# Delta rule by 64x64 tiles: the transpose of X comes from VectorE's block transpositions instead of products

## The reference, cut to what matters

```python
gcum = jnp.cumsum(g, axis=-1)
decay = jnp.exp(jnp.where(incl, gcum[..., :, None] - gcum[..., None, :], -jnp.inf))
kb = k * beta[..., None]
lower = jnp.where(strict, jnp.einsum('bhncd,bhnsd->bhncs', kb, k) * decay, 0.0)
tmat = lax.linalg.triangular_solve(eye + lower, eye, left_side=True, lower=True, unit_diagonal=True)
u = tmat @ (v * beta[..., None])
w = tmat @ (kb * jnp.exp(gcum)[..., None])
...
v_new = u_c - w_c @ s
o = qd_c @ s + a_c @ v_new
s * jnp.exp(gl_c)[..., None, None] + jnp.swapaxes(kd_c, -1, -2) @ v_new, o
```

## Time and profile before

| | us |
|---|---|
| median of 3 runs | 3926.3 |
| the runs | 3925.33 to 3931.67 |
| the profiled execution, its own time | 3924.58 |
| its span, first to last instruction | 3922.4 |
| the delta rule's chunks in it | 1394.3 to 1630, and a tail until 1640 |

### The profile page before, as it was taken

One profiled execution on the slowest core, in us unless ns is written; L12 is line 12 of the kernel. 1 busy time (PEld: TensorE's weight loads), 2 busy tenths in 40 slices (PEclk: granted clock), 3 DMA queues, 4 the chain that ended last, 5 costly groups with the idle time before them and its releaser, 6 DMA issues. The chain is left out here.

```text
span 3922.4 us, 55157 instructions
## 1 busy us (share of the span) xinstructions
PE 3588.2 (91%) x23086; PEld 2879.1 (73%) x23086; DVE 1959.0 (50%) x3107; ACT 844.8 (22%) x1650; POOL 1440.3 (37%) x701
## 2 busy tenths in 40 slices
PE   6897988999989978878999899899999899899998
PEld 3684567888877867757888576788888576788887
DVE  5797653223446444474233367863243377853342
ACT  3213512110011233201100344422000344421001
POOL 2331043226554223115455222235455222245454
PEclk9898999999999977889999899999999899999999
DMA  5443312212113100112332231123332322223322
GB/s 172 150 151 135 129 43 76 65 59 62 63 49 91 41 3 4 67 42 72 97 97 81 67 80 49 49 72 95 96 97 75 84 60 53 55 76 97 97 92 81
DMA packets 399811, 306.40 MB, mean 78 GB/s; under 512 B 11292, under 2 KB 367462, under 8 KB 398983
## 3 DMA queue, kind: packets, MB, share of 16 engines
q1 hardware_dynamic: 397464, 302.37, 25.6%
q10 hardware_dynamic: 2095, 0.44, 0.1%
HBM read 296.48 MB, written 6.29 MB: 77 GB/s over the span
## 5 line engine op out<-in xcount | busy, mean ns | idle before, releaser
L450 POOL TENSOR_TENSOR low<-raw,high 128x1024 fp32r<-128x1024 f32 (+1 forms) x437 | 1049.7, 2403 | 1828.6 <-DVE high L356 1828.6
L519 PE MATMUL scores<-high 128*128 128x512 f32 (+1 forms) x1944 | 743.1, 382 | 72.2 <-DVE low L704 31.8
L519 PE MATMUL scores<-low,high 128*128 128x512 f32 (+1 forms) x1944 | 729.4, 375 | 0.0
L519 PE MATMUL scores<-high,low 128*128 128x512 f32 (+1 forms) x1944 | 727.7, 374 | 0.0
L356 DVE CAST high<-raw 128x1024 fp32r<-128x1024 f32 (+1 forms) x437 | 394.4, 903 | 504.1 <-PE scores L519 261.1
L519 PE MATMUL bank<-high 128*128 128x512 f32 (+1 forms) x1480 | 541.6, 366 | 0.2
L519 PE MATMUL bank<-low,high 128*128 128x512 f32 (+1 forms) x1480 | 538.8, 364 | 0.0
L519 PE MATMUL bank<-high,low 128*128 128x512 f32 (+1 forms) x1480 | 538.1, 364 | 0.0
L519 PEld LDWEIGHTS scores<-high 128*128 128x128 f32 x1944 | 376.7, 194 | 154.7 <-POOL low L450 54.2
L519 PEld LDWEIGHTS scores<-high,low 128*128 128x128 f32 x1944 | 375.6, 193 | 65.9
L519 PEld LDWEIGHTS scores<-low,high 128*128 128x128 f32 x1944 | 377.2, 194 | 62.0 <-issue 1.0
(11 more groups left out here) (663 smaller groups left out, 5143.3 us busy)
## 6 DMA issues: line engine op xcount, KB each, us to landing
raw<-in_mlp_w SPq DMA_DIRECT2D x128, 512.0 KB, 3.9
raw<-in_w_in SPq DMA_DIRECT2D x76, 512.0 KB, 3.9
ring<-in_ada_w SPq DMA_DIRECT2D x32, 1024.0 KB, 7.5
raw<-in_w_gate SPq DMA_DIRECT2D x44, 512.0 KB, 3.8
raw<-in_w_up SPq DMA_DIRECT2D x44, 512.0 KB, 3.9
raw<-in_w_down SPq DMA_DIRECT2D x40, 512.0 KB, 3.5
mix<-in_ada_w SPq DMA_DIRECT2D x16, 1024.0 KB, 6.5
raw<-in_od_w_in SPq DMA_DIRECT2D x29, 512.0 KB, 3.9
```

The source lines that it names most:

```text
L450: pool.tensor_tensor(tile(low, u), tile(raw, u), tile(high, u).bitcast(F32), ALU.subtract)\
L519: mm = pe.matmul(out(p), stationary, moving, start=(k0 + k == 0 and i == 0), stop=(k0 + k == job.kc - 1 and i == len(pairs) - 1))
```

## The change

- Tiles of levels 0 to 4 are the two 64x64 blocks of the diagonal for each head in place of four of 32x32: 8 matmuls for a product. X, XT and `part` are 128x256 instead of 128x128, and so are the operations of VectorE that write all of them; the updates that `subtract` reads are 128x128 instead of 128x64. The masks and the identity become 64 wide (384 KB and 32 KB instead of 160 and 16).
- `second_turned` is gone at levels 1 to 4, and `subtract_turned` with it. In its place VectorE transposes X into XT by 32x32 blocks (`turn`) after each subtraction; until level 4 X has nothing outside the 32x32 blocks of the diagonal. X itself begins as VectorE's transposition of XT, so `second` at level 0 is gone.
- Level 5 is a level like the others, but keeps both updates: `part` on VectorE masks it, `second_turned` and `second` follow, and `subtract_turned` and `subtract` on VectorE.
- `square`, `wide`, `copy_part`, `copy_wide_part`, `place_square`, `place_corners` and `last_corner` are gone. ScalarE copies the two 64x64 blocks of each head into `inverse`, the part of level 6 and its corner.
- GpSimd's `place_blocks` is gone, and with it its waits for XT; three of GpSimd's waits for its own operations are gone, and `exponents` waits for an earlier `mask_decays`.
- VectorE's `advance` of both streams moves from behind `attention` to between the parts and the subtractions of level 5; `subtract_both` takes one stream after the other.

```diff
             def first(s, k, lv):
+                pe.wait_ge(s.xt_ready, 6 * k + lv)
+                for h in range(HEADS):
+                    for to, of in zip(halves, halves) if lv < 6 else ((s.earlier, s.later),):
+                        mm = pe.matmul(s.level[to, h, :], by_head(s.low)[of, h, to], s.XT[of, S(h)], start=True, stop=True)
+                mm.then_inc(s.firsts, 1)
...
             def second(s, k, lv):
-                if lv == 0:
-                    pe.wait_ge(s.part_ready, 5 * k + 1)
+                pe.wait_ge(s.part_ready, 6 * k + lv + 1)
+                pe.wait_ge(s.x_ready, 6 * k + lv)
                 for h in range(HEADS):
-                    for e, l in s.steps[0:1] if lv == 5 else ((b, b) for b in range(4)):
-                        mm = pe.matmul(s.level_x[R(l), h, :], s.part[R(e), B(h)], ident32[R(e), :] if lv == 0 else s.X[R(e), B(h)],
-                                       start=True, stop=True)
+                    for r in halves if lv < 5 else (s.earlier,):
+                        mm = pe.matmul(s.level_x[r, h, :], s.part[r, S(h)], s.X[r, S(h)], start=True, stop=True)
                 mm.then_inc(s.seconds, 1)
...
             def level(k, lv):
                 for s in both:
-                    second_turned(s, k, lv)
+                    if lv >= 5:
+                        second_turned(s, k, lv)
                     if lv < 6:
                         second(s, k, lv)
...
+            def copy_last_part(s, k):
                 act.wait_ge(s.firsts, 6 * k + 6)
+                act.activation(by_block(s.part)[s.earlier, :, :], s.level[s.earlier, :, :], ACT.Copy).then_inc(s.last_part, 1)
+
+            def place_blocks(s, k):
+                if k == 0:
+                    act.wait_ge(s.cleared, 2)
+                act.wait_ge(s.xt_ready, 6 * k + 6)
+                for r in halves:
+                    act.activation(by_head(s.inverse)[r, :, r], by_block(s.XT)[r, :, :], ACT.Copy).then_inc(s.diagonal, 1)
+
+            def place_corner(s, k):
+                act.wait_ge(s.seconds_turned, 2 * k + 2)
+                act.activation(by_head(s.inverse)[s.earlier, :, s.later], s.level_turned[s.earlier, :, :], ACT.Copy, scale=-1.0)\
+                    .then_inc(s.corner_ready, 1)
...
             def begin(s, k):
-                dve.wait_ge(s.seconds, 6 * k + 1)
-                if k:
-                    dve.wait_ge(s.square_ready, k)
-                dve.tensor_tensor(by_block(s.X), eye, s.level_x, ALU.subtract).then_inc(s.x_ready, 1)
+                dve.wait_ge(s.xt_ready, 6 * k + 1)
+                dve.transpose(s.X[:, :], s.XT[:, :]).then_inc(s.x_ready, 1)
+
+            def turn(s, k, lv):
+                dve.wait_ge(s.x_ready, 6 * k + lv + 1)
+                dve.transpose(s.XT[:, :], s.X[:, :]).then_inc(s.xt_ready, 1)
...
             def subtract_both(k, lv):
                 for s in both:
-                    subtract_turned(s, k, lv)
-                for s in both:
+                    if lv == 5:
+                        subtract_turned(s, k, lv)
                     subtract(s, k, lv)
+                    if lv < 5:
+                        turn(s, k, lv)
...
                     subtract_both(k, 4)
+                    for s in both:
+                        part(s, k, 5)
+                if has:
+                    for s in both:
+                        advance(s, j)
+                if more:
+                    subtract_both(k, 5)
                 if has:
                     for s in both:
                         attention(s, j)
-                        advance(s, j)
```

More of the change, by code:

```diff
@@ L2342 @@
         "query_raised": "ScalarE: of the queries (latent)", "keys_decayed": "ScalarE: keys decayed to the chunk's end",
-        "new_copied": "ScalarE: the new values", "square_ready": "ScalarE: X's blocks in the earlier 64 rows",
-        "wide_part": "ScalarE: the parts of levels 5 and 6 (2)", "corners": "ScalarE: corners of level 5 (3)",
+        "new_copied": "ScalarE: the new values", "last_part": "ScalarE: the part of level 6",
+        "corner_ready": "ScalarE: the corner of the inverse's last level", "diagonal": "ScalarE: blocks of the inverse (2)",
         "ends_ready": "VectorE: exponents", "low_ready": "VectorE: low",
-        "part_ready": "VectorE: the level's part of (X low) transposed (5: levels 0 to 4)",
-        "x_ready": "VectorE: X (5)", "xt_ready": "VectorE: X transposed (5)",
-        "xt_final": "VectorE: the corner of the inverse's last level", "attn_ready": "VectorE: attention (latent)",
+        "part_ready": "VectorE: the level's part of (X low) transposed (6: levels 0 to 5)",
+        "x_ready": "VectorE: X (6)", "xt_ready": "VectorE: X transposed (6)",
+        "attn_ready": "VectorE: attention (latent)",
         "rhs_ready": "VectorE: right-hand side", "state_ready": "VectorE: the state", "out_stored": "VectorE: the output (latent)",
@@ L2351 @@
         "values_scaled": "GpSimd: beta v", "decays_masked": "GpSimd: decays of the attention (latent)",
-        "query_ready": "GpSimd: decayed queries (latent)", "diagonal": "GpSimd: blocks of the inverse (4: later rows, earlier rows)",
-        "cleared": "GpSimd: the tiles that begin with zeros (3)"}
+        "query_ready": "GpSimd: decayed queries (latent)", "cleared": "GpSimd: the tiles that begin with zeros (2)"}
     def __init__(self, direction, banks, tiles, sems):
@@ L2369, in __init__ @@
         self.heads = slice(direction * HEADS, (direction + 1) * HEADS)
-        self.steps = [(0, 1), (2, 3)] if direction == 0 else [(3, 2), (1, 0)]
         self.earlier, self.later = (slice(0, 64), slice(64, P))[::1 if direction == 0 else -1]
         by_block = lambda t: t.rearrange("p (h n) -> p h n", h=HEADS)
-        self.level, self.level_turned = (by_block(self.level_bank[:, 128 * i:128 * i + 128]) for i in range(2))
-        self.level_x = by_block(self.gram_bank[:, 0:128])
-        self.corner = by_block(self.level_bank[:, 128:384])
+        self.level, self.level_turned = (by_block(self.level_bank[:, 256 * i:256 * i + 256]) for i in range(2))
+        self.level_x = by_block(self.gram_bank[:, 0:256])
     def sums_of(self, k):
@@ L2890, in last_corner @@
-            def last_corner(s, k):
-                dve.wait_ge(s.seconds_turned, 6 * k + 6)
-                dve.tensor_scalar(by_head(s.inverse)[s.earlier, :, s.later], s.corner[s.earlier, :, :], -1.0, None, ALU.mult)\
-                    .then_inc(s.xt_final, 1)
+                dve.wait_ge(s.seconds, 5 * k + lv)
+                dve.wait_ge(s.x_ready, 6 * k + lv)
+                rows = slice(0, P) if lv < 5 else s.earlier
+                own = s.half(s.X, lv, 0)[rows, :, :]
+                dve.tensor_tensor(own, own, s.half(s.gram_bank[:, 0:256], lv, 0)[rows, :, :], ALU.subtract).then_inc(s.x_ready, 1)
@@ L2986, in _ @@
                         lower(s, k + 1)
-                if more:
-                    for s in both:
-                        last_corner(s, k)
             for s in both:
```

171 lines of the change are left out of this document (43 added, 128 removed).

## The result

The kernel after takes 3878.76 us (median of 4 runs, 3873.06 to 3880.86), the kernel before 3928.99 beside it (3925.33 to 3932.06): ratio 0.987, 95% interval 0.9853 to 0.9887. A second comparison gave 0.9874, 0.9852 to 0.9897. It is 50 us faster; the forecast was 3901, 25 us faster.

The account below looks back on a forecast made before the run. TensorE was taken as bound by its work plus idle time from instruction supply and a lowered clock. Gaps -38, path +28 and clock -15 gave -25 us, so 3901 us, with a range of 3870 to 3930.

Parts of the forecast that it names:

- the band of 3886 to 3917: Whole kernel time in the main forecast outcome, given a chance of 0.62.
- The gaps: TensorE's "issue" idle time at 32x32 products, read as instruction supply: 38 of 39.1 us would go.
- the path: Time added in the delta rule by larger VectorE operations, transpositions and longer TensorE steps: 28 us.
- the clock's term: TensorE's half-level time, 2(1-share) times chunk length, 110 us in all, would fall by 45 us: -15 us.
- my price of 0.34: Chunk time per microsecond at half clock level, from comparing chunks 3 and 4 with the same work: 0.34 us.
- the clock goes to full nearly everywhere: Rival: TensorE's clock is full nearly throughout the chunks, clock term -37, kernel time 3879 us; chance 0.13.
- the level: One level with two 128x128 products between its halves: from 3.86 to 4.52 us, 0.66 more.
- The transposition itself: VectorE's transposition of 128x256 fp32 after each subtraction: taken as 0.42 us.
- The corner: ScalarE's corner copy at level 6, in three chunks without outputs: may come 0.5 us late, inside the 28.
- The advance of the state: VectorE's update between level 5's parts and subtraction: at most 1.7 us, hidden under TensorE's work.
- The signs named beforehand: Stage signs: "issue" under 5 us, 28 fewer transfers, chunks 34 to 36 us, share above 0.82, VectorE up a third.
- The signs of being wrong: Transposition waits over 1 us a level, clock share under 0.72, or 64x64 steps of 0.9 us.

Follow-up runs that it names:

- run 3: Kernel after plus 19 one-column matmuls before each `first` of levels 2 to 5 and `second` of levels 1 to 4, restoring the earlier record count: 3954.08 us.
- run 5: Kernel after with padding of 6 matmuls of 64 columns at each place where another version had 19 of one column: 3899.17 us.
- run 2: Kernel before, keeping 32x32 tiles, with VectorE's transpositions of X at levels 0 to 4 in place of products: 3866.89 us.
- run 4: Kernel after with every transposition of X into XT at levels 1 to 4 done twice, one after the other: 3901.29 us.
- run 6: Kernel after with ScalarE copying the inverse's blocks before the last level's part instead of after it: 3869.99 us.
- run 1: Kernel after's 64x64 tiles alone, with X's transpose still updated by products as in the kernel before: 3884.4 us.

## Why the prediction was right, and where its sizes were off

The measured time lies in the stated range of 3870 to 3930, but not in the band of 3886 to 3917 that had 0.62: the gain was twice the forecast one. The gaps and the path came out as summed; the clock's term was too small.

**The gaps (forecast -38).** Right. They are gone: 39.1 us on the lines of the earlier trace rows, 43.7 with the other tile products. That they are the supply of instructions I had read from counts; the traces now show it in time. The four gaps of TensorE in 17 us of the kernel before, and the DMA activity in slices of 0.425 us over the same 17 us:

```profile
1404.47 0.39 PE L2489 MATMUL bank<-XT,low 32*32 32x32 f32 x23 [1.83 <-issue]
...
1408.12 0.49 PE L2521 MATMUL bank<-X,part 32*32 32x32 f32 x21 [2.25 <-issue]
...
1412.01 0.54 PE L2521 MATMUL scores<-X,part 32*32 32x32 f32 x24 [1.76 <-issue]
...
1415.84 0.55 PE L2489 MATMUL bank<-XT,low 32*32 32x32 f32 x25 [1.91 <-issue]
```
```profile
DMA  1000000010000000020000000010000000010000
GB/s 39 0 0 0 0 0 0 0 39 0 0 0 0 0 0 0 0 39 0 0 0 0 0 0 0 0 39 0 0 0 0 0 0 0 0 39 0 0 0 0
...
q8 instruction: 5, 0.08, 2.1%
```

The transfers start at about 1402.0, 1405.4, 1409.2, 1413.1 and 1416.9 us, 3.4 to 3.9 us apart, and each gap ends 2.5 to 2.8 us after one starts. Runs 3 and 5 then show that the gaps come with the number of instructions, and run 3 that the rate counts and not the sum: with the records and transfers of before, in a stage 32 us longer, it has 10.3 us of gaps. A transfer brings about 128 matmul records (6,672 / 52), each with its weight load, so one in 3.6 us is 36 of them a microsecond. A level with two 128x128 products asks for 208 in 3.86 us before (54 a microsecond) and has the most gaps; 224 in 5.57 in run 3, with one product (40); 144 in 3.97 in run 2 (36), with few; and 80 in 4.79 after (17), with none. A short burst above the rate passes without a gap: 143 records in the 3 us of the first stretch shown in run 3 (48). The Trainium skill, "Runtime: NRT & Kernel Launch", instruction fetch mechanics, holds the fetch to be hidden; that is so for the kernel after and not for the 32x32 levels of before.

**The clock (forecast -15).** This is the mis-sized term. I took 45 us off the half-level time, on the ground that each level keeps 0.7 us of idle time. 89 went (110 to 21), at my price of 0.34 a gain of 30 us, and 40 us at 0.45, which is run 3's 39 / 86 if all that is left over there is clock. The rival "the clock goes to full nearly everywhere" had 3879, which is the time measured; the outcome is nearer to that rival than to the forecast. The step that failed is the one from idle time to clock. What I could not know, run 4 shows: waits of 0.45 to 0.9 us between bursts leave the clock at 1.00, while the waits of 1.6 us that run 6 takes away, the gaps of 2 us before and some gaps of 1 us (run 3) have a half-level stretch of several microseconds behind them. The Trainium skill, "TensorE: Matmul & The Clock Gate", section on oscillation, has the array throttled by waits between bursts: the longer waits here bear that out, the short ones do not. What separates a wait of 0.9 us in run 4 from the gap of 1.0 in run 3, and the one wait of 1.57 us in run 1 from its two others, stays open; so does why the gap of 1.61 us of the kernel before that ends at 1607.00 us has no such stretch behind it.

**The path (forecast +28).** -46.9 is -43.7 of gaps, -30 of clock and so +27 of path; with the clock at 0.45 it would be +37. The split between the two is no sharper than that. Its largest part is the level, 0.93 us longer, forecast 0.66 (4.79 for 4.52): the two `first` products took 1.27 us (1541.61 to 1542.88) where I had 0.92, since a 64x64 step is 0.51 us and not 0.46, and the second direction's starts 0.66 us after the first's, when its own transposition is done. That is 18.6 us in 20 levels, an estimate from the one level shown; the rest I have not parted. The transposition itself, at 0.445 us (0.416 at the beginning of a chunk) is within 0.03 of the 0.42 taken; the Trainium skill's 311 ns for 128x128 bf16 ("VectorE: DVE Perf Modes", three transpose paths) is met here by fp32 of that shape (312 ns in run 2), so to double it for 256 columns was the error of that estimate, not the figure. The waits for it are 0.40 us in most levels, 11.0 us in all, where the sum had 0.7 a level: from the first `second` to the first `first` it takes 1.54 us (forecast 1.60), but the two longer steps keep TensorE busy for 1.14 of them and not 0.92. The corner: a wait of 1.57 us in three chunks, where the kernel before waited 1.2 us for VectorE's corner (3.5 us in three waits): 0.4 late, forecast 0.5. Right in size, but I missed that in all three chunks, before and after, the clock falls behind this wait (run 6: 9.4 us for 4.2 us of waits). The advance of the state, moved ahead of level 5's subtraction, is hidden as forecast: TensorE waits 0.4 us in all for X ahead of the next chunk's grams.

**A reading of the earlier trace rows that was wrong.** I took the 0.61 us of the operation that begins XT, against 0.29 for a part of the size, for an excess that it always has. It is a mean over two kinds. Before, six of the twelve take 0.29 us and six 0.8 to 1.1; after, at 128x256, the shortest take 0.42. All six long ones before run beside a GpSimd operation of 128x512 (the first at 1509.53 us), but so does a short one after (1491.09 us), and no run was made to test it. It changed nothing in the sum.

**What the sum did not separate.** I gave both halves of the change one sum. Runs 1 and 2 part them: the transpositions alone make the stage 64.5 us shorter, the tiles alone 41.4, both together 46.9. With the transpositions in place the tiles of 64 remove 5.3 us of gaps and some clock and pay the longer path, 17.6 us net in the trace. The path term was nearly all theirs, and the prediction had no rival in which one half is a loss.

**The signs named beforehand.** Issue under 5 us: 0. 28 transfers fewer: 28. Share over 0.82: 0.95. VectorE up by a third: 33%. A chunk of 34 to 36 us: 33.7, just under, and 34.8 in the two full ones, 30.9 and 32.4 in the two before them, as the clock came back. The signs of being wrong did not show: TensorE waits 0.4 us a level for the transposition, and a 64x64 step is 0.51 us.

## What to carry to other kernels

Where a product is cut into many tiny matmuls, count instructions against time: in these runs, above some 36 fp32 matmul records a microsecond over a few microseconds TensorE waited for its instructions, and idle time with the releaser "issue" in the middle of alike instructions is the sign. Fewer instructions by an operation elsewhere (here a transposition of 0.3 to 0.45 us for 16 small products) can be worth more than larger tiles, whose products take longer. And price a wait of TensorE of over a microsecond at more than its length, about twice in run 6: look at the granted clock of the stretch behind it, and fill it with work that is due anyway.

## What the runs showed of the hardware that I had not expected

- Padding of 3,648 records of one column (11 ns each) made the kernel 75 us slower, 1,152 records of 64 columns (29 ns each) 20 us, in the same places. Number and columns both differ, so only the gaps (10.3 us against none) are shown to come with the number.
- The clock is more sensitive to one wait of over 1 us than to many of 0.45 to 0.9 us: it falls for 3 us or more behind ten of the twelve corner waits (1.1 to 1.6 us) of before, after and runs 1 and 2, and in run 4 behind two of the 47 waits for the transposed X, the two of over 1 us.
- VectorE transposes 128x128 fp32 by 32x32 blocks in 312 ns and 128x256 in 445 ns, hardly more than it takes to mask a tile of the size (288 and 421 ns).
- The VectorE operation that begins XT took 0.29 us in six of twelve cases before and 0.8 to 1.1 us in the six others, which all run beside a GpSimd operation of 128x512; why is not shown.
